# Who issues the hidden activations' trip through DRAM: SyncE's queue or GpSimd's

## The reference

```python
def swiglu(x, w_gate, w_up, w_down):
    return (jax.nn.silu(x @ w_gate) * (x @ w_up)) @ w_down

for l in range(DEPTH):                                  # DEPTH = 2
    x = layer_norm(ALPHA * x + 0.5 * swiglu(x, ffn1_...[l]), ...)
    x = layer_norm(ALPHA * x + hybrid_mixer(x, ...), ...)
    x = layer_norm(ALPHA * x + 0.5 * swiglu(x, ffn2_...[l]), ...)
```

## Time and profile before

| | |
|---|---|
| median of 3 runs | 1083.84 us (1083.62 to 1085.15) |
| profiled execution | 1083.67 us |
| its span | 1081.9 us (1.8 us lie around it) |
| TensorE busy in the span | 1072.1 us (99%), at a granted clock of 1.00 |
| VectorE, ScalarE, GpSimd busy | 772.0, 579.4, 137.3 us |
| second net of layer 0, of layer 1 | about 362 to 546, and 896 to 1075 us from the span's start |

### The profile page before, as it was taken

One profiled execution on the slowest core, in us unless ns is written; L12 is line 12 of the kernel. 1 busy time (PEld: TensorE's weight loads), 2 busy tenths in 40 slices (PEclk: granted clock), 3 DMA queues, 4 the chain that ended last, 5 costly groups with the idle time before them and its releaser, 6 DMA issues.

```text
span 1081.9 us, 14282 instructions
## 1 busy us (share of the span) xinstructions
PE 1072.1 (99%) x5197; PEld 882.7 (82%) x5197; DVE 772.0 (71%) x779; ACT 579.4 (54%) x641; POOL 137.3 (13%) x137
## 2 busy tenths in 40 slices
PE   8999999999999999999999999999999999999997
PEld 6888888888888788888888888888878887888886
DVE  5756557799979775555679665677999787655566
ACT  5755654768554544444456655547774546344441
POOL 1498000000000000000006970000000000000000
PEclk9999999999999999999999999999999999999999
DMA  8877879355566486777737877775455674688761
GB/s 285 263 216 231 296 223 225 105 184 171 175 185 208 149 272 226 233 259 225 250 124 231 248 244 254 230 199 165 148 166 157 195 268 133 209 268 270 235 208 40
DMA packets 192371, 226.39 MB, mean 209 GB/s; under 512 B 31540, under 2 KB 157128, under 8 KB 192328
## 3 DMA queue, kind: packets, MB, share of 16 engines
q1 hardware_dynamic: 192328, 225.83, 65.5%
HBM read 214.26 MB, written 11.53 MB: 209 GB/s over the span
## 4 chain that ended last, share of the span: by engine, by line
PE 97%; DMA 1%; SPq 1%; DVE 1%; issue 0%; ACT 0%; DVEq 0%
PE ps L578 25%; PE ps L555 19%; PE ps L557 18%; PE ps L556 18%; PE ps L538 4%; PE ps L540 2%; PE ps L974 1%; PE ps L976 1%; PE ps L975 1%; PE ps L593 1%; DMA raw<-in_ffn_w_up 1%; PE ps L901 1%; DMA tp<-in_ln_b 0%; PE ps L686 0%; PE ps L685 0%; PE ps L684 0%
## 5 line engine op out<-in xcount | busy, mean ns | idle before, releaser
L1449 DVE TENSOR_TENSOR w_lo<-raw,w_hi 128x2048 fp32r<-128x2048 f32 x172 | 399.9, 2329 | 166.7 <-ACT w_hi L1058 165.6
L1058 ACT CAST w_hi<-raw 128x2048 fp32r<-128x2048 f32 x172 | 328.1, 1910 | 162.1 <-PE ps L578 78.9
L555 PE MATMUL ps<-w_hi,xT 128*128 128x512 f32 x848 | 331.8, 391 | 0.3 <-DVE w_lo L1461 0.2
L556 PE MATMUL ps<-w_lo,xT 128*128 128x512 f32 x848 | 330.1, 389 | 0.0
L557 PE MATMUL ps<-w_hi,xT 128*128 128x512 f32 x848 | 330.1, 389 | 0.0
L555 PEld LDWEIGHTS ps<-w_hi,xT 128*128 128x128 f32 x848 | 159.2, 188 | 36.2 <-issue 2.5
L557 PEld LDWEIGHTS ps<-w_hi,xT 128*128 128x128 f32 x848 | 159.2, 188 | 33.0
L556 PEld LDWEIGHTS ps<-w_lo,xT 128*128 128x128 f32 x848 | 159.2, 188 | 32.7
L578 PE MATMUL ps<-w_hi,rows_hi 128*128 128x512 f32 x396 | 126.6, 393 | 0.0
L578 PE MATMUL ps<-w_hi,rows_lo 128*128 128x512 f32 x396 | 125.4, 390 | 0.0
L578 PE MATMUL ps<-w_lo,rows_hi 128*128 128x512 f32 x396 | 125.2, 389 | 0.0
(11 more groups left out here) (248 smaller groups left out, 1117.1 us busy)
## 6 DMA issues: line engine op xcount, KB each, us to landing
raw<-in_ffn_w_down SPq DMA_DIRECT2D x44, 1024.0 KB, 6.6
raw<-in_ffn_w_gate SPq DMA_DIRECT2D x86, 512.0 KB, 4.1
raw<-in_ffn_w_up SPq DMA_DIRECT2D x86, 512.0 KB, 5.2
raw<-in_w_in SPq DMA_DIRECT2D x30, 1024.0 KB, 5.1
hid_dram<-qT SPq DMA_DIRECT2D x160, 64.0 KB, 2.8
qT<-hid_dram SPq DMA_DIRECT2D x40, 256.0 KB, 2.6
raw<-in_w_out SPq DMA_DIRECT2D x8, 1024.0 KB, 4.9
raw<-in_w_in SPq DMA_DIRECT2D x8, 512.0 KB, 5.0
```

Source lines behind the costliest of these rows:

```text
L555: mm(o, xT[:, c, 0, tok], h, start=c == UPPER_FIRST[0], stop=False, skip_group_check=True)
L556: mm(o, xT[:, c, 0, tok], w, start=False, stop=False, skip_group_check=True)
L1058: nc.scalar.copy(w_hi[s][:, :], raw[s][:, :]).then_inc(hi_made.sem, 1)
L1449: tt(w_lo[s][:, :], raw[s][:, :], f32(w_hi[s][:, :]), ALU.subtract).then_inc(lo_made.sem, 1)
```

## The change

In the second net of each layer the four writes and the read-back are taken out of SyncE's queue and issued by GpSimd, ten times in each layer, between the two norms at which GpSimd has work. The waits stay the same: for the transposed blocks before the writes, for the writes before the read-back. They count on two semaphores of their own, and ScalarE's cast waits for the one of the net that it is in. The first net of each layer keeps its turn in SyncE's queue.

```diff
-            def turn_hidden(l, n):
+            def turn_hidden(l, f, n):
+                if f:
+                    return
                 sp.wait_ge(blocks_made.sem, blocks_made.at(l, n))
...
-                    turn_hidden(l, f * (STEPS - 1) + i - 1)
+                    turn_hidden(l, f, i - 1)
...
-                turn_hidden(l, (f + 1) * (STEPS - 1))
+                turn_hidden(l, f, STEPS - 1)
...
-            def hidden_hi(l, n, spare=False):
-                sc_.wait_ge(h_turned.sem, h_turned.at(l, n))
+            def hidden_hi(l, f, n, spare=False):
+                turned = pool_turned if f else h_turned
+                sc_.wait_ge(turned.sem, turned.at(l, n))
...
+            def turn_hidden(l, n):
+                pool.wait_ge(blocks_made.sem, blocks_made.at(l, STEPS - 1 + n))
+                for a in range(4):
+                    nc.gpsimd.dma_start(hid_dram.rearrange("g i a r -> a i g r")[a],
+                                        hid_blocks[32 * a:32 * a + 32, :].rearrange("i (g r) -> i g r", g=4)
+                                        ).then_inc(pool_out.sem, 16)
+                pool.wait_ge(pool_out.sem, pool_out.at(l, n))
+                nc.gpsimd.dma_start(hid_turned, hid_dram.rearrange("g i a r -> (g i) (a r)")).then_inc(pool_turned.sem, 16)
...
                 deviations(l, 1)
+                for n in range(1, STEPS):
+                    turn_hidden(l, n)
                 deviations(l, 2)
```

More of the change, by code:

```diff
@@ L226, in trunk @@
         blocks_made = Events(sem("blocks_made"), 2 * (STEPS - 1))
-        blocks_out = Events(sem("blocks_out"), 2 * (STEPS - 1), unit=64)
-        h_turned = Events(sem("h_turned"), 2 * (STEPS - 1), unit=16)
+        pool_out = Events(sem("pool_out"), STEPS - 1, unit=64)
+        pool_turned = Events(sem("pool_turned"), STEPS - 1, unit=16)
+        blocks_out = Events(sem("blocks_out"), STEPS - 1, unit=64)
+        h_turned = Events(sem("h_turned"), STEPS - 1, unit=16)
         h_hi = Events(sem("h_hi"), 2 * (STEPS + 1))
@@ L1126, in step @@
                     split(l, k0 + i * 3 + 1, 1, LANDED[k0 + 1] + i * 16)
-                    hidden_hi(l, b0 + i)
+                    hidden_hi(l, f, i)
                     split(l, k0 + i * 3 + 2, 2, LANDED[k0 + 2] + i * 32)
@@ L1141, in ffn @@
                     split(l, k0 + FFN_CHUNKS - 2)
-                hidden_hi(l, b0 + STEPS - 1, final)
+                hidden_hi(l, f, STEPS - 1, final)
                 split(l, k0 + FFN_CHUNKS - 1)
```

## The result

The median went from 1083.73 us (4 runs, 1083.57 to 1085.15) to 1100.04 us (4 runs, 1098.17 to 1108.19): a ratio of 1.0161, 95% interval 1.0143 to 1.0179. The profiled execution took 1099.41 us; its span is 1097.6 us, 15.7 us more than before.

The account below looks back on a forecast made before the run. TensorE, busy 1072.1 of 1081.9 us, was taken as the bound; new waits of 2.9, 3.0 and 2.3 us, together 8.2 us, led to a forecast of 1092.0 us, range 1084.0 to 1110 us.

Parts of the forecast that it names:

- the sum: New TensorE waits in the second nets: 2.9, 3.0 and 2.3 us, other blocks 0, together 8.2 us.
- the three sites: First block of each layer's second net and last block of layer 1: new TensorE waits of 2.9, 3.0 and 2.3 us.
- The limits: Longest transposition-to-cast times without TensorE waiting: first blocks 7.3 us, layer 1's last block 6.25 us, middle blocks 10.2 us.
- trip: Second nets, from the end of VectorE's block transposition to ScalarE's cast; 6.36 us before at layer 0's first block.
- VectorE holds GpSimd up: Rival: VectorE's subtractions delay GpSimd's issues in second nets; 1099 us at three places alone, up to 1123 us; chance 0.10.
- growth: Second nets: lengthening of transposition-to-cast time by five issues on GpSimd at 1.0 us instead of SyncE's 2.17 us; 2.8 us.
- crowding: Second nets: read-back's landing stretched by loads now running beside it; taken as 1.0 us, none at the last block.
- cover: Slack before TensorE waits: 0.93 and 0.82 us at the first blocks, 0.51 us at layer 1's last block.
- The other blocks: Blocks between first and last in second nets: transposition to cast 9.5 us, under 10.2 us, costing 0.
- the 6.1 us: Middle blocks of second nets: fixed time from ScalarE's cast to the end of the next block's transposition, 6.1 us.
- every step waits: Rival: at 1302 ns or more an issue, middle blocks exceed 10.2 us; 1109 us, or 1095 us without crowding; chance 0.15.

Follow-up runs that it names:

- experiments 1: Changed kernel with the first block of each second net back on SyncE's queue, the other nine on GpSimd; median 1096.3 us, ratio 1.0118.
- experiment 5: Changed kernel with ten products into an unused bank put on TensorE ahead of each second net's first down products; median 1098.02 us.
- experiment 6: Changed kernel with an added GpSimd drain right behind its last turn; four executions from 1092.42 to 1104.49 us, median 1098.77 us.
- experiment 3: Kernel before the change, with one unneeded 128 KB transfer issued by GpSimd ahead of layer 0's second net; 1084.08 us, ratio 0.9993.
- experiment 4: Changed kernel with SyncE's queue holding the loads behind the turn until the read-back has landed; median 1100.07 us, ratio 1.0144.
- experiment 9: Changed kernel with an early GpSimd drain and SyncE holding the `w_down` load until the block's read-back has landed; 1089.99 us, ratio 1.0054.
- experiment 2: Changed kernel with only the first block of each second net on GpSimd, the other nine on SyncE's queue; median 1093.93 us, ratio 1.0087.

## Why the prediction was right in sign and wrong in size

The sign was right and the time lay in the range; the value was 8 us too low, and the 8.2 us of the sum stand against 16.3 in the medians, 15.7 in the profile. The step that failed is the sum: "Together 8.2 us of new waits on TensorE" holds nothing but waits. The waits at the three sites measured 6.0 us; the slower clock behind two of them (3.4 us) and GpSimd's closing drain (4.3 us), both put at nothing, make up most of the rest.

**Right.** TensorE is the bound, SyncE's freed queue brought nothing, and the new waits came at the three sites named. The limits were right to 0.1 us: the first blocks pay trip less limit (10.17 - 7.29 = 2.88; layer 1: 9.68 - 7.28 = 2.40, measured 2.39), and middle steps pay trip + 6.09 less 16.32. The rival by which VectorE holds GpSimd up is refuted: no write took more than 742 ns.

**Right by luck: the first trips.** They were forecast at 10.2 us from an issue of 1.0 us (growth 2.8) and crowding of 1.0. Measured in layer 0: five issues take 2.96 instead of 2.17 us, growth 0.8, and from the end of the read-back's issue to the cast it is 5.22 instead of 2.25 us, crowding 3.0. The two errors cancel at the first blocks, and only there. At the last block, which has no loads beside it, the trip is 7.04 us, the wait 0.69 instead of 2.3. I had argued that the read-back is spared because it doesn't stand behind the loads in one queue. In the Trainium skill the page "DMA: Bandwidth & Descriptors", section "Issuing engines are not separate DMA queues", says the opposite: transfers run on the same 16 engines and interleave, whoever issued them. The traces agree with it, 5.80 us beside loads and 2.93 without. The order that SyncE's one queue gave, read-back first and loads behind, was worth 3 us. The growth of 0.8 us that I had worked out as an estimate from the same page's section Specifications was nearer than my 2.8: at the last block, without loads, the trip grew by 1.30 us (start of the writes 0.26, issue of the five 0.60, wait for the landing 0.34, read-back 0.10).

**Failed: a wait costs its length.** The sum priced the first blocks by trip less cover alone. The clock's fall behind the wait cost 1.72 us more at each, 3.4 in all; experiments 1 and 5 show it. It need not follow: in experiment 6 the first blocks waited 2.33 and 2.31 us and the clock stayed at 1.00.

**Failed: "The two new semaphores and the two waits of GpSimd cost nothing: behind them on GpSimd is only `rstd`".** Behind them is also the closing drain, which grew with the number of transfers: 4.3 us, shown by experiments 3 and 6.

**Failed in part: "The other blocks: ... under 10.2, 0".** In the profiled execution the middle trips of 8.9 to 9.7 cost nothing, as forecast. In others a net stays above the limit and costs 11 to 14 us. I treated the trip as one number; it depends on when the loads beside it leave. The rows had a sign of it: the cast at 945.82, from which I took the 6.1 us, ends a trip of 10.72 us in the kernel before, since that block was transposed at 935.10; I had priced the middle blocks by the 5.74 us of the last one, which has no loads beside it. The rival "every step waits" had the limit and the price of a step right, but a cause (1.3 us an issue) that isn't there. The changed kernel's own highest execution, 1108.19 us, fits a late net; it was not traced.

**The accounts of the 15.7 us.** Waits at the three sites 2.88 + 2.39 + 0.69 = 6.0; lower clock 3.4; drain 4.3; layer 1's first net 1.2, where SyncE's issue of `c_in` took up to 6.12 us instead of 4.07, the turn behind it came late, and TensorE waited 0.9 us for it. That net isn't changed, and the change does not force the 1.2 us: from `rstd` to `rstd` (545.15 to 720.58 before) it took 175.4 us before and in experiments 4, 5, 6 and 9, which also move all turns, 176.6 here, and 175.9 in experiment 3, the kernel before with one transfer. The remaining 0.8 us of the second nets is not assigned.

## What to carry to other kernels

A queue is also an order: before an issue is moved to another engine, list what stood behind it and now runs beside it, and price the transfer by rows with and without such company. Where TensorE has no slack, price a wait by the wait and by the slower products behind it, and look at what an engine must still finish when the program ends. Where a margin is thin, take the spread of a duration over the phases of its neighbours, not one value, and time the kernel often enough to see two groups.

## What the runs showed of the hardware

- At the first blocks, waits of 2.39 to 2.94 us of a TensorE that had been busy throughout were followed by a lower granted clock over the next 4 us, 0.58 and 0.67 in the changed kernel, 0.57 and 0.64 in experiment 2; waits there of 2.33 and 2.31 us (experiment 6) and of 1.65 and 1.62 (experiment 9), or the time filled with products (experiment 5), by 1.00. At the last `hid` of experiment 4 a wait of 2.94 us left it at 1.00, so the length of the one wait doesn't decide alone.
- GpSimd's drain takes about 82 ns for each transfer that its queue has issued, 1.09 to 9.29 us from none to 100, long after the last of them has landed. Once done early, it is short at the end.
- A write of 128 pieces and 64 KB takes GpSimd 0.55 us to issue (SyncE 0.43), and landing is not quicker for it: at the last block of layer 1, with no loads beside, the writes are there 1.65 us after the end of the last issue, against 1.31 from SyncE; at layer 0's first block 1.66 against 1.91.
